# One core, two model blocks: another order of modulation, norms and first products, up to the attention heads

## The chip, the cores and the metric

The kernel runs as one program on one core of a Trainium2 chip. The metric is device time in microseconds, lower is better. Engines are named as in the profile: PE (TensorE, with PEld for its weight loads), ACT (ScalarE), DVE (VectorE), POOL (GpSimd), SP (SyncE, which issues all DMAs here).

## The reference, cut to what matters

The program runs two different blocks of a transformer on 256 tokens of width 1024, all in float32. Only the start of the first block is touched:

```python
sh1, sc1, g1, sh2, sc2, g2 = adaln(c, mod_w[0], mod_b[0])      # silu(c) @ mod_w + mod_b, 6 x 1024
csh1, csc1, *_ = adaln(c_ctx, mod_w[0], mod_b[0])
a  = rms_norm(x, g) * (1 + sc1) + sh1                          # 256 x 1024
ac = rms_norm(ctx, g) * (1 + csc1) + csh1                      # 256 x 1024
q, k, v, p = split(a @ w_in, [512, 640, 768])                  # 512, 128, 128, 512 wide
kc, vc = split(ac @ w_in[:, 512:768])                          # keys and values of the context
q = rope(rms_norm_per_head(q)); k = rope(rms_norm_per_head(k)); kc = rms_norm_per_head(kc)
y = concat(attend(q, [kc; k], [vc; v]), multiscale_pool(p)) @ w_out
x = x + g1 * y; x = x + g2 * hier_moe(modulate(x, sh2, sc2))
```

## The kernel before, in words

**Weights.** Every chunk of weights is 128 partitions x 2048 float32 (1 MiB; 0.5 MiB for a chunk of keys and values). SP walks the chunks in the order in which PE uses them and issues one DMA for each into a ring of seven slots (five during the heads); from the eighth chunk on each issue waits until PE has read the chunk that held the slot. Small inputs are issued at fixed places of that walk (`sync`, `c.n` is the number of the chunk).

**Exact products.** Apart from modulation, a product of a float32 activation with a float32 weight is done as three products of rounded parts (`mm3`): ACT writes the high part of the weights (`a_split`, tile `hi`), DVE or POOL subtracts it from the raw chunk to get the low part (`v_split`, `g_split`, tile `lo`), and the activation is split in the same way into `hTh` and `hTl` (for the context `yTh`, `yTl`). Chunks of `q` are subtracted on DVE, those of `kv` and `p` on POOL.

**Modulation.** A piece (layer, p) is 512 columns of `mod_w`: two chunks, 32 small products on PE into one bank (`t_mod`), a copy by ACT to `acc` (`a_mod`), a transposition back on PE (`t_mod_T`), and an addition of the bias on DVE (`v_mod`, for a gate `v_gate`). Pieces (0,0) to (0,3) are needed first; eleven others (`MODS0`) are computed between the products of the attention heads, step by step, in bank 3.

**A norm.** ACT squares and sums the rows (`a_stats`), DVE computes 1/rms by ten small steps on the tile `st` and puts it on a diagonal (`v_diag`), PE multiplies the input by that diagonal, which turns it too (`t_norm`), and DVE and ACT scale, shift and split the four result banks by turns (`v_norm`, `a_norm`; POOL takes one low part, `g_norm`).

**Order.** Every engine's program is written out by hand in `tensor`, `scalar`, `vector`, `gpsimd` (lines 3134 to 3312), and each engine executes strictly in order. Before, PE does modulation, the norm of x (`a0x`), the norm of the context (`a0c`), then the products kv, q, p, then turns queries and keys (`t_qk`) and enters the 16 heads (`t_heads0`). On DVE `v_keys0` (norm and rotation of the keys) stands ahead of `v_queries0`.

**Banks.** PSUM has eight banks. A product takes its banks by turns from a pool of banks (`POOLS`: A is 0 to 3, B is 4 to 7, S is 0 to 2). Its first product into a bank waits until the last reader of that bank has emptied it (`free`). All products of this stage came from pool B before: kv took banks 4 to 7, q banks 4 and 5, p banks 6 and 7.

Of the kernel before, what the change touches and what calls it, by code (L numbers as in the profile page):

```python
# [44 lines left out]
SMALL = ("sil", "cst", "col", "x", "cx", "row", "pos", "gb00", "gb01", "gb10", "gb11", "fg")  # L45
# [260 lines left out]
MODS0 = (0, 4), (0, 5), (0, 6), (0, 7), (0, 8), (0, 9), (1, 0), (1, 1), (1, 2), (0, 10), (0, 11)  # L306
EXTRA = {8: (1, 4), 10: (1, 5)}, {8: (1, 11)}
MODS = [(0, 0), (0, 1), (0, 2), (0, 3), *MODS0, (1, 3), *EXTRA[0].values(), (1, 6), (1, 7), (1, 8), (1, 9), (1, 10),
# [102 lines left out]
class Net(Tiles):  # L411
# [8 lines left out]
    def sync(self, s, book):  # L420
# [11 lines left out]
        for c in book.order:  # L432
            if c.n == 0:
                small("sil", self.sil[:, :], self.t_in["colp"][:, 160:176])
            elif c.n == 2:
                small("cst", self.cst[:, :], self.t_in["cst"])
            elif c.n == 4:
                small("col", self.col[:, :], self.t_in["colp"])
                small("x", self.x[:, :, :], self.t_in["x"])
                small("cx", self.cx, self.t_in["ctx"])  # L440
            elif c.n == 10:
                small("row", self.row[:, :], rows(0, RKEEP))
                small("pos", self.posi[:, :], self.t_in["pos"])
# [117 lines left out]
    def t_mod_T(self, t, l, p, pool="B"):  # L561
# [4 lines left out]
        t.wait_ge(*t.at("in", "cst"))  # L566
# [9 lines left out]
    def v_mod(self, v, l, p, cdst=None):  # L576
# [8 lines left out]
        v.wait_ge(*v.at("in", "col"))  # L585
# [65 lines left out]
    def v_diag(self, v, name, buf, c0):  # L651
        self.v_stats(v, name, c0)
        r = self.st[:, c0 + 4:c0 + 6]
        v.wait_ge(*v.at("in", "cst"))
# [259 lines left out]
    def a_queries0(self, a):  # L914

        for t in range(2):
            b = a.bank("q", t)
            a.wait_ge(*a.at("keys 0"))
# [37 lines left out]
    def a_qk(self, a):  # L956
        qT, kT = self.qk()
        a.wait_ge(*a.at("used", ("p", 1)))
# [172 lines left out]
    def t_mods0(self, t):  # L1131

        steps, late = None, []
        for n in range(self.STEPS0 + 6):
            for i in self.turn0(n):
# [4 lines left out]
                if i % 9 == 8:  # L1140
                    late.append((n + 2, piece))
# [12 lines left out]
    def v_mods0(self, v):  # L1154
        late = []
# [84 lines left out]
    def t_shift_of(self, t, l):  # L1240

        t.wait_ge(*t.at("scale", l, 1))
        b = t.take("B", "router shift", l)
# [20 lines left out]
    def t_route(self, t, l, src, beside):  # L1264
# [24 lines left out]
        gk = self.r3(64, 8)  # L1289
        t.wait_ge(*t.at("group marks", l))  # L1290
# [1843 lines left out]
    def tensor(self, t):  # L3134
# [37 lines left out]
    def scalar(self, a):  # L3172
        H, Y = self.H3, self.Y3
        self.a_silu(a)
        self.a_stats(a, "a0x", self.x, lambda h, t: a.at("in", "x"), self.s1, 0, ("sil",))
        self.a_stats(a, "a0c", self.cx, lambda h, t: a.at("in", "cx"), self.s2, 32)
        for p in range(4):
            self.a_mod(a, 0, p)
        self.a_split(a, "kv", 0, ahead=1)
        self.a_norm(a, "a0x", self.cadj[:, 3, :], self.mcol[:, 0:8], self.hT, H, [("scale", 0, 0)], [])  # L3180
        self.a_norm(a, "a0c", self.cadj[:, 2, :], self.cadj[:, 0, :], self.hTc(), Y, [("scale c",)], [])
        self.a_split(a, "kv", 1)
        self.a_split(a, "q", 1)
# [41 lines left out]
    def vector(self, v):  # L3225
        H, Y = self.H3, self.Y3
        self.v_silu(v)
        self.v_diag(v, "a0x", self.s1, 0)
        self.v_diag(v, "a0c", self.s2, 32)
        for p in range(4):  # L3230
            self.v_mod(v, 0, p, self.cadj[:, p // 2, 4 * (p % 2):4 * (p % 2) + 4])
        v.wait_ge(*v.last)
# [18 lines left out]
        self.v_queries0(v)  # L3251
# [3 lines left out]
        self.v_split(v, "eo", 0, 1, ahead=1)  # L3255
# [225 lines left out]
```

## Time and profile before

| | us |
|---|---|
| three runs | 1717.47, 1702.03, 1711.02 (median 1711.02) |
| profiled execution | 1706.65, of it span 1704.9 |
| first product of kv on PE | at 44.18 |
| turning of queries and keys on PE | at 79.06 |
| heads on PE | 81.38 to 172.13 |
| PE busy over the span | 93% |

Times inside the profiled execution are counted from the start of its span. The first block's attention ends at 172.13 us; the other 1530 us run code that the change doesn't touch. A row of the timeline gives the start, the time from the first start to the last end, the engine, the line, the tiles (out<-in), the number of instructions, and in brackets how long the engine had been idle before and what released it. Several rows of the same kind are merged.

### The profile page before, as it was taken

What the parts mean: (1) busy time and instruction counts of PE and PEld (TensorE: products, weight loads), DVE (VectorE), ACT (ScalarE), POOL (GpSimd) and SP (SyncE); (2) the same over time, 40 slices, a digit from 0 to 9 for tenths busy, and PEclk for the clock granted to TensorE, in tenths of its full rate; (3) what the DMA queues carried; (4) which work ended last, traced back from release to release, by engine and by line L of the source; (5) the groups of instructions that cost most, each with busy time, mean ns of one, the idle gap of its engine ahead of it and who ended that gap; (6) DMA issues with size and microseconds to landing.
All of it is one profiled execution on the core that took longest, in us unless ns stands there. A gap on an engine that the chain in (4) does not pass through costs nothing.

```text
span 1704.9 us, 23882 instructions
## 1 busy us (share of the span) xinstructions
PE 1588.9 (93%) x9950; PEld 1323.7 (78%) x9950; DVE 764.7 (45%) x1477; ACT 682.4 (40%) x1024; POOL 435.2 (26%) x163
## 2 busy tenths in 40 slices
PE   4999979999898899989999889999999998899997
PEld 4856867775797678668888668999888886789996
DVE  2722578422766774253352373522433522645222
ACT  3323367432435664233223344444432223354442
POOL 1200015330000343223100025655531000246543
PEclk7989889999998899999999999999999999999999
DMA  9578169769643696754433234555543332256550
GB/s 386 186 253 301 41 252 353 295 222 366 269 144 142 238 345 238 252 220 141 148 115 149 75 143 153 189 185 186 166 153 135 136 133 90 103 171 208 180 190 26
DMA packets 46620, 327.26 MB, mean 192 GB/s; under 512 B 5424, under 2 KB 5424, under 8 KB 8752
## 3 DMA queue, kind: packets, MB, share of 16 engines
q1 hardware_dynamic: 46512, 325.73, 53.0%
q8 instruction: 79, 1.29, 0.3%
q14 instruction: 29, 0.24, 0.0%
HBM read 324.66 MB, written 1.05 MB: 191 GB/s over the span
## 4 chain that ended last, share of the span: by engine, by line
PE 79%; DVE 13%; ACT 3%; DMA 2%; issue 1%; POOL 1%; DVEq 0%; SPq 0%; ACTq 0%
PE ps L201 28%; PE ps L204 16%; PE ps L206 16%; PE ps L205 16%; DVE lo L212 5%; DMA raw<-in_wmod 2%; ACT hi L209 1%; PE ps L2624 1%; DVE ar L212 1%; DVE big L220 1%; POOL lo L212 1%; DMA raw<-in_wo_v 1%; DVE gl L212 1%; DVE ar L2675 1%; DVE xn L212 0%
## 5 line engine op out<-in xcount | busy, mean ns | idle before, releaser
L212 POOL TENSOR_TENSOR lo<-raw,hi 128x2048 fp32r<-128x2048 f32 (+2 forms) x76 | 354.3, 4672 | 656.9 <-ACT hi L209 656.9
L209 ACT ACTIVATE hi<-raw 128x2048 fp32r<-128x2048 f32 (+2 forms) x192 | 350.8, 1858 | 47.5 <-PE ps L206 12.4
L212 DVE TENSOR_TENSOR lo<-raw,hi 128x2048 fp32r<-128x2048 f32 (+1 forms) x116 | 291.2, 2528 | 99.7 <-ACT hi L209 99.4
L201 PE MATMUL ps<-hT,raw 128*128 128x256 f32 x1024 | 231.4, 382 | 0.0
L201 PEld LDWEIGHTS ps<-hT,raw 128*128 128x128 f32 x1024 | 191.0, 190 | 29.6 <-issue 4.0
L204 PE MATMUL ps<-hTh,hi 128*128 128x256 f32 x640 | 183.1, 286 | 5.4 <-DVE hTl L212 2.9
L205 PE MATMUL ps<-hTl,hi 128*128 128x256 f32 x640 | 182.4, 285 | 0.0
L206 PE MATMUL ps<-hTh,lo 128*128 128x256 f32 x640 | 182.3, 285 | 0.0
L204 PEld LDWEIGHTS ps<-hTh,hi 128*128 128x128 f32 x640 | 124.1, 194 | 7.2 <-issue 3.5
L204 PE MATMUL ps<-hi,hTh 128*128 128x512 f32 (+3 forms) x320 | 119.5, 373 | 10.6 <-DVE hTl L212 5.2
L205 PEld LDWEIGHTS ps<-hTl,hi 128*128 128x128 f32 x640 | 124.1, 194 | 0.5
L206 PEld LDWEIGHTS ps<-hTh,lo 128*128 128x128 f32 x640 | 124.1, 194 | 0.0
L204 PE MATMUL ps<-hi,gh 128*128 128x512 f32 x256 | 106.5, 416 | 12.4 <-DVE lo L212 12.4
L206 PE MATMUL ps<-hi,hTl 128*128 128x512 f32 (+3 forms) x320 | 117.6, 367 | 0.0
L205 PE MATMUL ps<-lo,hTh 128*128 128x512 f32 (+3 forms) x320 | 117.4, 367 | 0.0
L212 POOL TENSOR_TENSOR big<-big 128x512 f32<-128x512 f32 x16 | 20.3, 1269 | 343.8 <-DVE big L220 343.8
L212 DVE TENSOR_TENSOR fTl<-s,fTh 128x512 fp32r<-128x512 f32 x32 | 22.1, 692 | 190.8 <-ACT fTh L209 190.8
L206 PE MATMUL ps<-hi,gl 128*128 128x512 f32 x256 | 103.6, 405 | 0.0
L205 PE MATMUL ps<-lo,gh 128*128 128x512 f32 x256 | 103.5, 404 | 0.0
L204 PE MATMUL ps<-hi,fTh 128*128 128x512 f32 x256 | 99.8, 390 | 0.0
L205 PE MATMUL ps<-lo,fTh 128*128 128x512 f32 x256 | 99.8, 390 | 0.0
L206 PE MATMUL ps<-hi,fTl 128*128 128x512 f32 x256 | 99.6, 389 | 0.0
(295 smaller groups left out, 2551.9 us busy)
## 6 DMA issues: line engine op xcount, KB each, us to landing
raw<-in_wgu SPq DMA_DIRECT2D x64, 1024.0 KB, 4.9
raw<-in_wmod SPq DMA_DIRECT2D x48, 1024.0 KB, 5.5
raw<-in_wdn SPq DMA_DIRECT2D x32, 1024.0 KB, 5.2
raw<-in_wgt SPq DMA_DIRECT2D x32, 1024.0 KB, 4.9
raw<-in_wup SPq DMA_DIRECT2D x32, 1024.0 KB, 4.7
raw<-in_wdown SPq DMA_DIRECT2D x32, 1024.0 KB, 5.1
raw<-in_wz SPq DMA_DIRECT2D x12, 1024.0 KB, 4.9
raw<-in_wbr SPq DMA_DIRECT2D x8, 1024.0 KB, 5.7
```

Source lines behind the costliest of these rows:

```text
L201: return self.e.matmul(o, l, r, start=first, stop=last)
L204: self.e.matmul(o, l[0], r[0], start=first, stop=False)
L205: self.e.matmul(o, l[0], r[1], start=False, stop=False)
L206: return self.e.matmul(o, l[1], r[0], start=False, stop=last)
L209: return self.e.activation(o, a, f, **kw)
L212: return self.e.tensor_tensor(o, a, b, op)
L220: return self.e.scalar_tensor_tensor(out=o, in0=a, scalar=s, in1=b, op0=op0, op1=op1)
L2624: m = t.e.transpose(ps[:, b, 128 * h:128 * h + 128], pb[:, n * h + 128 * kt:n * h + 128 * kt + 128], self.C("ident"))
L2675: o = v.e.tensor_tensor_reduce(pb[:, n * h:n * h + n], ps[:, b[h % 2], n * (h // 2):n * (h // 2) + n], mask(i, n), 1.0, -3e38, ALU.add, AL ...
```

## The change

Six things are moved, all in the first block:

1. Small inputs: only the identity (64 KB of `cst`) and the modulation's bias (80 KB of `col`) are loaded early, as `id` and `col0`; the rest of both is loaded after the chunks of kv, with the row constants and gates. The context (1 MiB, as x) is loaded at chunk 10.
2. ACT copies modulation pieces 0 and 1 before it squares x, and squares the context only after the second chunk of q is split; DVE's `v_diag` calls follow.
3. PE computes q directly after the norm of x, in banks 0 and 1 (pool A), then the norm of the context, then kv.
4. DVE does `v_queries0` before it copies the results of kv out of PSUM; `v_keys0` comes last. POOL splits the chunks of kv and p, DVE those of q.
5. Two gate pieces, (0,4) and (0,5), are computed by `t_mod` between p and `t_qk` (`AHEAD0`); `MODS0` keeps nine. Their transpositions stay in the heads.
6. After the heads DVE splits one chunk of the output weights before the last tail, not two, and the router's shift takes a bank of pool S.

```diff
-MODS0 = (0, 4), (0, 5), (0, 6), (0, 7), (0, 8), (0, 9), (1, 0), (1, 1), (1, 2), (0, 10), (0, 11)
+AHEAD0 = (0, 4), (0, 5)
+MODS0 = (0, 6), (0, 7), (0, 8), (0, 9), (1, 0), (1, 1), (1, 2), (0, 10), (0, 11)
...
             elif c.n == 2:
-                small("cst", self.cst[:, :], self.t_in["cst"])
+                small("id", self.cst[:, 0:128], self.t_in["cst"][:, 0:128])
+                small("col0", self.col[:, 0:160], self.t_in["colp"][:, 0:160])
             elif c.n == 4:
-                small("col", self.col[:, :], self.t_in["colp"])
                 small("x", self.x[:, :, :], self.t_in["x"])
+            elif c.n == 10:
                 small("cx", self.cx, self.t_in["ctx"])
-            elif c.n == 10:
+            elif c.n == 12:
+                small("cst", self.cst[:, 128:], self.t_in["cst"][:, 128:])
+                small("col", self.col[:, 160:], self.t_in["colp"][:, 160:])
                 small("row", self.row[:, :], rows(0, RKEEP))
...
     def tensor(self, t):
         self.t_norm(t, "a0x", self.x, self.s1)
+        both = [(H, ("hT", "a0x"), 0), (H, ("hT", "a0x"), 1)]
+        self.t_rows(t, ("q",), ("q",), 512, both, "A")
         self.t_norm(t, "a0c", self.cx, self.s2)
-        both = [(H, ("hT", "a0x"), 0), (H, ("hT", "a0x"), 1)]
         self.t_rows(t, ("kv",), ("kv",), 256, both + [(Y, ("hT", "a0c"), 0), (Y, ("hT", "a0c"), 1)])
-        self.t_rows(t, ("q",), ("q",), 512, both)
         self.t_rows(t, ("p",), ("p",), 512, both)
+        for piece in AHEAD0:
+            self.t_mod(t, *piece)
...
     def scalar(self, a):
         self.a_silu(a)
-        self.a_stats(a, "a0x", self.x, lambda h, t: a.at("in", "x"), self.s1, 0, ("sil",))
-        self.a_stats(a, "a0c", self.cx, lambda h, t: a.at("in", "cx"), self.s2, 32)
         for p in range(4):
             self.a_mod(a, 0, p)
+            if p == 1:
+                self.a_stats(a, "a0x", self.x, lambda h, t: a.at("in", "x"), self.s1, 0, ("sil",))
+        self.a_split(a, "q", 0, ahead=0)
+        self.a_norm(a, "a0x", self.cadj[:, 3, :], self.mcol[:, 0:8], self.hT, H, [("scale", 0, 0)], [])
+        self.a_split(a, "q", 1, ahead=0)
+        self.a_stats(a, "a0c", self.cx, lambda h, t: a.at("in", "cx"), self.s2, 32)
         self.a_split(a, "kv", 0, ahead=1)
-        self.a_norm(a, "a0x", self.cadj[:, 3, :], self.mcol[:, 0:8], self.hT, H, [("scale", 0, 0)], [])
         self.a_norm(a, "a0c", self.cadj[:, 2, :], self.cadj[:, 0, :], self.hTc(), Y, [("scale c",)], [])
-        self.a_split(a, "kv", 1)
-        self.a_split(a, "q", 1)
         self.a_queries0(a)
+        self.a_split(a, "p", 0, ahead=1)
...
     def vector(self, v):
+        self.v_split(v, "q", 0, ahead=0)
         self.v_norm(v, "a0x", self.cadj[:, 3, :], self.mcol[:, 0:8], self.hT, H, [("scale", 0, 0)], [])
+        self.v_split(v, "q", 1, ahead=0)
+        self.v_diag(v, "a0c", self.s2, 32)
         self.v_norm(v, "a0c", self.cadj[:, 2, :], self.cadj[:, 0, :], self.hTc(), Y, [("scale c",)], [])
         self.v_turns0(v)
-        self.v_split(v, "kv", 1)
         for k in range(4):
             v.wait_ge(*v.at("hT", "a0c", k))
+        self.v_queries0(v)
         for i in range(4):
             b = v.bank("kv", i)
...
         self.v_keys0(v)
-        self.v_queries0(v)
```

PE, the first product of each group with its waits, from the norm of the context to `t_qk`, before (`hi_83` and `hi_84` are kv's chunks, `hi_85` and `hi_86` q's, `hi_87` and the second `hi_83` p's; `free4` is bank 4):

```order
L204 MATMUL ps<-hi_83,hTh 128x256 [waits s_dve,s_free4,s_lo_pool]
...
L204 MATMUL ps<-hi_85,hTh 128x512 [waits s_free4,s_lo_dve]
...
L204 MATMUL ps<-hi_85,hTh 128x512 [waits s_free5]
...
L204 MATMUL ps<-hi_87,hTh 128x512 [waits s_free6,s_lo_pool]
...
L953 MATMUL ps<-cst,z 128x128 [waits s_dve,s_free4]
```

The same engine and place now (`hi_83` and `hi_84` are q's chunks, `hi_85` and `hi_86` kv's, `hi_87` p's first):

```order
L204 MATMUL ps<-hi_83,hTh 128x512 [waits s_dve,s_lo_dve]
...
L201 MATMUL ps<-s_65,z 128x128 [waits s_free4,s_dve]
...
L204 MATMUL ps<-hi_85,hTh 128x256 [waits s_free4,s_lo_pool]
...
L204 MATMUL ps<-hi_87,hTh 128x512 [waits s_free4,s_lo_pool]
...
L204 MATMUL ps<-hi_87,hTh 128x512 [waits s_free5]
...
L201 MATMUL ps<-raw_69,sil 32x128 [waits s_raw0,s_free6]
...
L957 MATMUL ps<-cst,z 128x128 [waits s_dve,s_free4]
```

q waits for no bank any more, and p, which follows kv directly, now waits for banks 4 and 5, the two that kv has just filled.

DVE, from the rotation tables to the last keys or queries, before:

```order
L212 TENSOR_TENSOR rt<-cst,row 128x4x16 x2
L212 TENSOR_TENSOR lo_79<-raw_72,hi_85 128x2048
L212 TENSOR_TENSOR lo_80<-raw_73,hi_86 128x2048
L223 COPY z<-ps 128x256 x4
L212 TENSOR_TENSOR s_62<-z 128x256 x2
L226 TENSOR_REDUCE st<-s_62 128x4 x2
...
L212 TENSOR_TENSOR s_65<-ps,rt 128x512
L212 TENSOR_TENSOR s_65<-ps,rt 128x8x16 x4
L212 TENSOR_TENSOR z<-s_65 128x512
```

And now:

```order
L212 TENSOR_TENSOR rt<-cst,row 128x4x16 x2
L212 TENSOR_TENSOR s_65<-ps,rt 128x512
L212 TENSOR_TENSOR s_65<-ps,rt 128x8x16 x4
L212 TENSOR_TENSOR z<-s_65 128x512
...
L226 TENSOR_REDUCE st<-s_62 128x8 x2
...
L216 TENSOR_SCALAR st<-st 128x16 x2
L223 COPY z<-ps 128x256 x4
L212 TENSOR_TENSOR s_62<-z 128x256 x2
```

The four copies `z<-ps` empty the banks of kv. They stood directly behind the split of q's chunks; now all of `v_queries0` stands ahead of them.

## Rows read from the trace of the kernel before

**Rows 1.** Stages by windows: PE, PEld, DVE, ACT, POOL busy, PE clock, DMA share, GB/s.

```profile
0.00:44.18 44.18, 21.07 (x325) 17.51 (x325) 12.57 (x49) 14.46 (x33) 7.02 (x7) 0.81 0.96 387
44.18:79.06 34.88, 34.88 (x193) 31.07 (x194) 29.19 (x67) 13.17 (x15) 11.36 (x3) 0.95 0.57 208
81.38:172.13 90.75, 85.46 (x996) 55.48 (x996) 21.89 (x54) 28.59 (x66) 0.00 (x0) 0.92 0.79 267
```

**Rows 2.** The chain that ended last, start and duration, up to the first kv product.

```profile
1.20 5.48 DMA raw<-in_wmod
...
8.79 24.52 DMA raw<-in_wmod
...
42.41 1.76 issue
```

**Rows 3.** DMA issues of the first 150 us: size, median time to landing.

```profile
col<-in_colp SPq DMA_DIRECT2D x1, 803.0 KB, 13.5
cst<-in_cst SPq DMA_DIRECT2D x1, 568.0 KB, 8.5
```

**Rows 4.** ACT by timeline: squares of x, modulation copies, high parts.

```profile
20.92 0.63 ACT L209 ACTIVATE s<-x 128x512 f32<-128x512 f32 x1 [18.12 <-DMA x<-in_x]
...
26.68 0.42 ACT L209 ACTIVATE acc<-ps 128x128 f32<-128x128 f32 x2
...
48.51 7.31 ACT L209 ACTIVATE hi<-raw 128x2048 fp32r<-128x2048 f32 x4
```

**Rows 5.** DVE by timeline: the norm of x, q's low parts.

```profile
36.17 1.00 DVE L217 TENSOR_SCALAR hT<-ps,cadj,mcol 128x256 f32<-128x256 f32 x2 [0.46 <-PE ps L201]
37.93 0.79 DVE L212 TENSOR_TENSOR hTl<-hT,hTh 128x512 fp32r<-128x512 f32 x1 [0.76 <-ACT hTh L209]
...
50.45 4.50 DVE L212 TENSOR_TENSOR lo<-raw,hi 128x2048 fp32r<-128x2048 f32 x2 [0.64 <-ACT hi L209]
```

**Rows 6.** PE by timeline: the context's norm, two products of p.

```profile
38.58 3.83 PE L201 MATMUL ps<-s,z 128*128 128x128 f32 x32
...
72.02 0.39 PE L206 MATMUL ps<-hi,hTl 128*128 128x512 f32 x1
...
78.82 0.39 PE L206 MATMUL ps<-hi,hTl 128*128 128x512 f32 x1
```

**Rows 7.** DVE and POOL by timeline, where both work at once.

```profile
54.10 10.08 POOL L212 TENSOR_TENSOR lo<-raw,hi 128x2048 fp32r<-128x2048 f32 x2 [6.42 <-ACT hi L209]
...
57.46 0.42 DVE L223 COPY z<-ps 128x256 f32<-128x256 f32 x1 [1.02 <-PE ps L206]
58.02 6.44 DVE L212 TENSOR_TENSOR s<-z 128x256 f32<-128x256 f32 x2
...
1076.40 9.50 POOL L212 TENSOR_TENSOR lo<-raw,hi 128x2048 fp32r<-128x2048 f32 x2 [4.36 <-ACT hi L209]
...
1076.76 4.58 DVE L212 TENSOR_TENSOR st<-st 128x2 f32<-128x2 f32 x1
1081.38 4.55 DVE L217 TENSOR_SCALAR st<-st 128x2 f32<-128x2 f32 x1
```

**Rows 8.** DVE by timeline: second query tile, reductions, last factors.

```profile
73.92 1.48 DVE L212 TENSOR_TENSOR s<-ps,rt 128x512 f32<-128x512 f32 x5
...
76.04 1.27 DVE L226 TENSOR_REDUCE st<-s 128x8 f32<-128x512 f32 x2
...
79.44 0.25 DVE L216 TENSOR_SCALAR st<-st 128x16 f32<-128x16 f32 x2
```

**Rows 9.** Windows with PE at half its clock.

```profile
44.00:48.00 4.00, 3.82 (x19) 3.85 (x20) 2.61 (x5) 3.74 (x8) 1.28 (x1) 0.57 1.01 426
...
109.00:123.00 14.00, 14.00 (x114) 8.10 (x106) 2.02 (x6) 3.21 (x7) 0.00 (x0) 0.51 0.49 163
```

**Rows 10.** PE in the heads, by form and by timeline: modulation's products.

```profile
L201 PE MATMUL ps<-raw,sil 128*32 128x128 f32 x704 | 30.5, 295 | 5.3 <-ACT acc L209 5.3
...
86.05 1.52 PE L201 MATMUL ps<-raw,sil 128*32 128x128 f32 x48
```

More of the change, by code:

```diff
@@ L44 @@
 SEMS.update({f"raw{r}": f"a chunk of weights landed in slot {r}" for r in range(NR)})
-SMALL = ("sil", "cst", "col", "x", "cx", "row", "pos", "gb00", "gb01", "gb10", "gb11", "fg")
+SMALL = ("sil", "id", "cst", "col0", "col", "x", "cx", "row", "pos", "gb00", "gb01", "gb10", "gb11", "fg")
 SEMS.update({f"in_{k}": f"{k} landed" for k in SMALL})
@@ L301, in source @@
     return part(t_in["wdown"][at[0], at[1]], at[2]), "pool"
-MODS0 = (0, 4), (0, 5), (0, 6), (0, 7), (0, 8), (0, 9), (1, 0), (1, 1), (1, 2), (0, 10), (0, 11)
+AHEAD0 = (0, 4), (0, 5)
+MODS0 = (0, 6), (0, 7), (0, 8), (0, 9), (1, 0), (1, 1), (1, 2), (0, 10), (0, 11)
 EXTRA = {8: (1, 4), 10: (1, 5)}, {8: (1, 11)}
-MODS = [(0, 0), (0, 1), (0, 2), (0, 3), *MODS0, (1, 3), *EXTRA[0].values(), (1, 6), (1, 7), (1, 8), (1, 9), (1, 10),
+MODS = [(0, 0), (0, 1), (0, 2), (0, 3), *AHEAD0, *MODS0, (1, 3), *EXTRA[0].values(), (1, 6), (1, 7), (1, 8), (1, 9), (1, 10),
         *EXTRA[1].values()]
@@ L565, in t_mod_T @@
         t.wait_ge(*t.empty("mod", l, p))
-        t.wait_ge(*t.at("in", "cst"))
+        t.wait_ge(*t.at("in", "id"))
         t.wait_ge(*t.free(b))
@@ L584, in v_mod @@
         pv = self.ps[:, b, 0:128].rearrange("p (q w) -> p q w", q=4)
-        v.wait_ge(*v.at("in", "col"))
+        v.wait_ge(*v.at("in", "col0"))
         v.wait_ge(*v.full("mod T", l, p))
@@ L653, in v_diag @@
         r = self.st[:, c0 + 4:c0 + 6]
-        v.wait_ge(*v.at("in", "cst"))
+        v.wait_ge(*v.at("in", "id"))
         v.wait_ge(*v.last)
@@ L917, in a_queries0 @@
             b = a.bank("q", t)
-            a.wait_ge(*a.at("keys 0"))
+            a.wait_ge(*a.at("diag used", "a0x"))
             a.wait_ge(*a.full("q", t))
@@ L957, in a_qk @@
         qT, kT = self.qk()
-        a.wait_ge(*a.at("used", ("p", 1)))
+        a.wait_ge(*a.at("used", ("mod", *AHEAD0[-1], 1)))
         for i in (5, 4, 0, 1, 2, 3):
@@ L1075, in t_pool0 @@
         t.wait_ge(*t.at("landed", c.key))
+        t.wait_ge(*t.at("in", "col"))
         for g in range(0, 4, 2):
@@ L1131, in t_mods0 @@
     def t_mods0(self, t):
-        steps, late = None, []
+        steps, late = None, [(2 + i, piece) for i, piece in enumerate(AHEAD0)]
         for n in range(self.STEPS0 + 6):
@@ L1140, in t_mods0 @@
                 if i % 9 == 8:
-                    late.append((n + 2, piece))
+                    late.append((n + 3, piece))
             for at, piece in late:
@@ L1154, in v_mods0 @@
     def v_mods0(self, v):
-        late = []
+        late = [(2 + i, piece) for i, piece in enumerate(AHEAD0)]
         for n in range(self.STEPS0 + 6):
@@ L1242, in t_shift_of @@
         t.wait_ge(*t.at("scale", l, 1))
-        b = t.take("B", "router shift", l)
+        b = t.take("B" if l else "S", "router shift", l)
         rw = self.K("rw", 160 * l, 160).rearrange("p (k n) -> p k n", k=8)
@@ L1289, in t_route @@
         gk = self.r3(64, 8)
+        t.wait_ge(*t.at("in", "cst"))
         t.wait_ge(*t.at("group marks", l))
@@ L3188, in scalar @@
             a.ac(self.z[:, t, 768:1280], self.ps[:, b, :]).then_inc(*a.up(f"free{b}"))
+        for piece in AHEAD0:
+            self.a_mod(a, *piece)
         self.a_qk(a)
@@ L3227, in vector @@
         self.v_silu(v)
-        self.v_diag(v, "a0x", self.s1, 0)
-        self.v_diag(v, "a0c", self.s2, 32)
         for p in range(4):
             self.v_mod(v, 0, p, self.cadj[:, p // 2, 4 * (p % 2):4 * (p % 2) + 4])
+            if p == 1:
+                self.v_diag(v, "a0x", self.s1, 0)
         v.wait_ge(*v.last)
@@ L3254, in vector @@
         self.v_shares0(v, 1)
-        self.v_split(v, "eo", 0, 1, ahead=1)
+        self.v_split(v, "eo", 0, 1, ahead=0)
         self.v_tail0(v, 1)
@@ L3285, in gpsimd @@
         H, Y = self.H3, self.Y3
+        self.g_norm(g, "a0x", self.hT, H)
         self.g_split(g, "kv", 0, ahead=1)
-        self.g_norm(g, "a0x", self.hT, H)
         self.g_norm(g, "a0c", self.hTc(), Y)
-        self.g_split(g, "kv", 1)
-        self.g_split(g, "q", 1)
+        self.g_split(g, "p", 0, ahead=1)
         self.g_moe(g, 0, "a1")
```

## The prediction

> **What bounds the kernel now.** I read the windows first, cut at the places where PE's work changes kind, then the chain of waits from the start, then the timelines of ACT, DVE, POOL and PE. The change touches only the time up to 172.13 us. Three stages lie in it [rows 1]. Up to 44.18 us PE is busy for 21 of 44 us and the DMA engines for 0.96: this stage waits for weights. From 44.18 to 79.06 us (kv, q, p) PE is busy without a gap. In the heads, 90.75 us, PE is busy for 85.5. So the first stage can be shortened by loading less, the second only by removing work or by starting it earlier, the third by removing PE's work. After 172.13 us nothing is moved but one split on DVE and one bank, and I expect no difference there.
>
> The chain says what starts the second stage: the last modulation chunk lands at 8.79 + 24.52 = 33.3 us, PE works on it and on two norms, and then stands for 1.76 us [rows 2]. That stand is the wait for bank 4, which DVE empties late.
>
> **Part 1, loads.** The first chunk landed at 6.7 us, the eighth at 33.3 [rows 2], and with four small inputs (x and the context among them, 1 MiB each) 10.3 MiB lay between them: 2.57 us per MiB. Ahead of the eighth chunk the change removes 504 KB of constants and 723 KB of columns [rows 3] and 1024 KB of context, 2.2 MiB: it should land at 27.7 us, 5.6 us earlier, and q's first chunk, now next in line, at 30.2. ACT no longer holds the modulation copies behind eight squares (20.92 to 26.68 us [rows 4]); that alone is worth nothing, as the copies still wait for the last chunk. The constants that come late (keys' and queries' tables) follow kv's chunks: 4.1 + 2.57 for each of the 15.2 MiB up to the row constants is 43 us, and they are first used near 61. No cost; if that cover went, DVE's `v_turns0` would stand.
>
> **Part 2, the start of q.** High part of q's first chunk 1.83 us (a quarter of 7.31 [rows 4]), low part 2.25 (half of 4.50), DVE's scaling and split of the first bank 2.55 (36.17 to 38.72 [rows 5]): 30.2 + 6.6 = **36.8 us**, against 44.18 for kv before. Gain so far 7.4 us.
>
> **Part 3, q.** From 72.02 to 78.82 us PE started 30 products [rows 6]: 0.227 us each, 48 are 10.9 us. The stand before it will cost clock: before, PE stood 1.76 us and then showed a granted clock of 0.57 from 44 to 48 us [rows 2, 9], half speed (1.2 instead of 2.4 GHz) for about 3.4 us, so 1.7 us lost. I take the same here: q ends at 36.8 + 12.6 = 49.4.
>
> **Part 4, the context's norm, which now stands between q and kv.** ACT ends x's norm about 5.6 us after DVE began it (39.9), splits q's second chunk (1.83) and squares the context (eight squares took 5.76 us [rows 4], four 2.9): 44.7 us. DVE then needs ten small steps and two diagonals, 2.7 us, so 47.4, ahead of the end of q. But ACT's next work is the high parts of kv, and POOL starts to subtract about 1.1 us later, at 45.8, twice 2.5 us. Here rows 7 decide. At 58.02 us two DVE operations that read two SBUF tiles took 6.44 us, where their kind needs 0.3 each; POOL's two subtractions ended at 64.18. At 1076.76 us a step on two columns took 4.58 us and the next one 4.55, one for each of POOL's two subtractions, while the copy out of PSUM at 57.46 took 0.42 under the same load. So each POOL subtraction lets one DVE step through and holds the next to its end. Ten small steps against two subtractions: the diagonal comes at 45.8 + 5.1 + 1.2 = 52.1 us, and PE stands **2.7 us**. Then the norm, 3.83 us [rows 6] and 1.7 for the clock after the stand: 57.6. Then kv, 96 products of half the columns, 11.5 us: 69.1. The bounds of the stand are 0 (DVE done before POOL begins) and 5.1 (both subtractions in full).
>
> The Trainium skill (SBUF — State Buffer, "SBUF: two separate sides") states the same as an exclusive lock between VectorE and GpSimd, held for a whole instruction, for VectorE operations with two SBUF inputs or in a 2-port mode. By it a reduction of one tile in float32 would pass under POOL. No row shows one under load; I let it pass, and otherwise 1.3 us [rows 8] would have to be added below.
>
> **Part 5, the wait of p for its banks.** This is the largest term. PE's rows show that p now takes banks 4 and 5, just filled by kv, and DVE's rows that the copies which empty them stand behind `v_queries0`. DVE ends the context's low parts at 60.7 us and the tables at 61.3. Queries: tile 0 2.2 us (63.5), products of tile 1 1.5 us (65.0) [rows 8]. ACT has meanwhile squared q and written p's high part (61.1 + 1.8), and POOL's two subtractions of p, 4.5 us each when alone (9.50 for two [rows 7]), run from 63.5 to about 68.0 and, after DVE has slipped in once (0.7), to 73.1. DVE: the addition of tile 1 waits to 68.0, ends 68.7; reductions 1.3, 70.0; the first step on `st` waits to 73.1; the rest 2.4 us (77.31 to 79.69 before), 75.5; the first copy 0.4: **75.9 us**. PE finished kv at 69.1, so it stands 6.8 us. Bounds: without the lock DVE is there at 69.8 (0.7 us of standing); with the reductions held too, 8.1. I take the middle, as rows 7 show the same operations on the same POOL chunks. p: 10.9 + 1.7 for the clock, 88.5. p's low parts (73.1) are there in time.
>
> **Part 6, the two pieces.** 48 products of modulation took 1.52 us [rows 10], or 64 for a piece 2.0 us: 4.0 us more ahead of `t_qk`, **92.5** against 79.06, +13.4. Keys (7 us of DVE from 77) are done by 85. In the heads the same 4.0 us go, and of four stands behind ACT's copy of bank 3, 5.3 us [rows 10], which hit the pieces whose last step falls into the first third of a round, three are left: -1.3. Half-speed stretches there (109 to 123 us [rows 9]) I leave as they are. The first chunk for the heads is requested when (0,4) has been used, about 10 us before it is needed, and lands in some 5.5. DVE's split of the second output chunk moves behind the tail and is needed 5 us later than it is ready: nothing.
>
> **Sum.** From q's start to `t_qk`: q 12.6, stand 2.7, norm 5.5, kv 11.5, stand 6.8, p 12.6, pieces 4.0, together 55.7 us, against 34.9 before: +20.8. Less 7.4 for the earlier start: +13.4. Less 5.3 in the heads: **+8.1 us**. Against the profiled execution, 1706.65, that is 1714.8. The median of the three runs lies 4.4 above it, the mean of all four times 2.7 above; I say **1716**.
>
> **The rivals.** (B) DVE is through in time: POOL's subtractions of p come late or let DVE through, and p starts with 0.7 us of standing. Less 6.1 and 1.7 of clock: +0.3, about 1707 to 1711. For it: a shift of 2 us in ACT's order is enough to separate the two engines. Against: both start from the same event, the end of the context's norm. (C) Faster: neither stand occurs (-2.7 and -1.7 more, so -4), and the stretch of 14 us at half clock in the heads, which began soon after a stand of 1.6 us, doesn't come, as fewer stands are left: -7. Together -11, 1696 to 1700. It decides if no PE stand over 1.1 us is left in the heads: the ones of that length did not bring the clock down. (D) Slower: the stand of p lasts 8.1 us and the half clock after it 14 us, as in the heads [rows 9], not 3.4: 1.3 and 5.3 more, +14.7, 1721 to 1726. It decides if p's products are still at half speed when the pieces begin. (E) The heads don't shorten, because each round is bound by the chain score, maximum, exponential and not by PE: +4 on the forecast, 1720. Against it: in rows 1 PE idles only 5.3 of 90.75 us, all named.
>
> **How the numbers follow.** Forecast 0.50, B 0.24, C 0.10, D 0.09, E 0.07. One per cent is 17 us, about what a measurement tells from no change; all cases but the ends of C and D lie within it: faster 0.03, same 0.91, slower 0.06. The runs of before spread over 15 us, and the range takes in B, E and most of D: 1703 to 1725.
>
> **What would show it.** Right: q's first product near 37 us; a DVE step on `st` of over 2 us near 46 to 51; PE idle 5 to 8 us ahead of p's first product, ended by a DVE copy `z<-ps`; `t_qk` near 92; heads about 5 us shorter. Wrong: q later than 40 (loads not bound by bytes), no gap ahead of p (B), a heads stage as long as before (E).

## The result, and the profile after

The changed kernel takes **1715.11 us** (median of 19 runs, 1704.7 to 1741.23); the kernel before, run beside it, 1705.32 (19 runs, 1695.37 to 1717.47). The ratio is 1.0053 (95%: 1.0034 to 1.0073): half a per cent slower, inside the one per cent called no change, at the place forecast (1716). Every ratio here and in the table below leaves out runs more than 1.5% above the fastest of their kernel (three of the changed kernel's 19, up to six of twelve below); medians, ranges and means have all runs. The profiled execution took 1709.32 us, of it span 1707.5, against 1706.65 and 1704.9.

The first rows are those of the start: DMA and ACT in the chain of waits, and PE's timeline (start, duration, what, and in brackets the idle time before and its releaser).

```profile
1.67 7.55 DMA raw<-in_wmod
...
11.25 19.07 DMA raw<-in_we_q
30.35 1.92 ACT hi L209
```

```profile
27.88 1.08 PE L201 MATMUL ps<-raw,rt 128*32 128x128 f32 x32 [1.02 <-DMA raw<-in_wmod]
...
37.08 0.77 PE L204 MATMUL ps<-hi,hTh 128*128 128x512 f32 x1 [3.82 <-DVE hTl L212]
...
44.27 0.50 PE L204 MATMUL ps<-hi,hTh 128*128 128x512 f32 x1 [0.15 <-DVE lo L212]
...
51.91 3.84 PE L201 MATMUL ps<-s,z 128*128 128x128 f32 x32 [1.87 <-DVE s L216]
...
75.64 0.77 PE L204 MATMUL ps<-hi,hTh 128*128 128x512 f32 x1 [8.38 <-DVE z L223]
...
89.15 3.70 PE L201 MATMUL ps<-raw,sil 128*32 128x128 f32 x128
92.78 1.62 PE L957 MATMUL ps<-cst,z 128*128 128x128 f32 x12
94.89 3.69 PE L201 MATMUL ps<-raw,z 128*128 128x256 f32 x16 [0.48 <-ACT big L209]
...
178.34 1.91 PE L201 MATMUL ps<-col,mcol 128*128 128x20 f32 x16
```

The eighth chunk is used at 27.88 (33.3 before, [rows 2]), q's first chunk lands at 30.3, q starts at 37.08. Then come two stands (stretches in which PE waits): 1.87 us ahead of the context's norm, ended by the diagonal (`s`), and 8.38 us ahead of p, ended by a copy `z<-ps`. `t_qk` is at 92.78, the heads end at 178.34; before, 79.06 and 172.13.

DVE under those two stands, and POOL beside it (same columns):

```profile
45.80 2.41 DVE L212 TENSOR_TENSOR st<-st 128x2 f32<-128x2 f32 x1
48.24 2.31 DVE L220 SCALAR_TENSOR_TENSOR st<-st 128x2 f32<-128x2 f32 x1
50.59 0.16 DVE L212 TENSOR_TENSOR st<-st 128x2 f32<-128x2 f32 x1
...
61.68 4.99 DVE L212 TENSOR_TENSOR z<-s 128x512 f32<-128x512 f32 x1
66.80 1.48 DVE L212 TENSOR_TENSOR s<-ps,rt 128x512 f32<-128x512 f32 x5
68.32 3.28 DVE L212 TENSOR_TENSOR z<-s 128x512 f32<-128x512 f32 x1
71.52 1.27 DVE L226 TENSOR_REDUCE st<-s 128x8 f32<-128x512 f32 x2
...
75.08 1.41 DVE L223 COPY z<-ps 128x256 f32<-128x256 f32 x4
```

```profile
45.79 4.75 POOL L212 TENSOR_TENSOR lo<-raw,hi 128x1024 fp32r<-128x1024 f32 x2 [6.65 <-ACT hi L209]
...
61.49 9.55 POOL L212 TENSOR_TENSOR lo<-raw,hi 128x2048 fp32r<-128x2048 f32 x2 [3.77 <-ACT hi L209]
```

This is the pattern of [rows 7] again. One step on two columns normally takes 0.16 us (the row at 50.59); while POOL's two small subtractions ran, two such steps took 2.41 and 2.31. Ahead of p two additions, one for each of POOL's large subtractions, took 4.99 and 3.28.

By windows (PE, PEld, DVE, ACT, POOL busy, then PE clock, DMA share, GB/s):

```profile
0.00:44.00 44.00, 25.71 (x316) 19.95 (x316) 12.97 (x36) 15.60 (x30) 1.48 (x5) 0.88 0.96 388
...
66.00:76.00 10.00, 1.62 (x12) 1.44 (x11) 9.45 (x24) 0.00 (x0) 5.05 (x2) 0.73 0.31 106
75.00:79.00 4.00, 3.36 (x8) 2.71 (x9) 3.68 (x14) 0.00 (x0) 0.00 (x0) 0.50 0.01 4
...
178.00:1707.50 1529.50, 1441.38 (x8432) 1215.02 (x8431) 703.28 (x1304) 623.83 (x906) 414.74 (x153) 0.97 0.51 182
```

In the first 44 us PE now does 25.7 us of work instead of 21.1 [rows 1]. In ten microseconds around the second stand it does 1.6, and the granted clock after it is 0.50 (1.2 GHz). The span moved less than the heads' end (2.6 against 6.2 us): the stage behind the heads, in which only one split and one bank were moved, took 1529.2 us instead of 1532.8. Windows at the same place behind the heads say why, first before, then after:

```profile
174.00:181.00 7.00, 6.39 (x18) 4.77 (x17) 6.96 (x7) 4.92 (x4) 0.00 (x0) 0.51 0.31 126
```

```profile
180.00:187.00 7.00, 6.25 (x31) 5.06 (x31) 6.97 (x7) 4.71 (x4) 0.00 (x0) 1.00 0.36 136
```

Seven microseconds at the same place, before at half clock, now at full clock (18 products against 31): about 3.5 us. I don't count them for the change: in the fourteen profiled executions of the table below the stage behind the heads took 1528.5 to 1538.1 us, and in the eight that have the changed code there 1528.5 to 1535.7. With one execution of each this is likely, not shown.

Every run also has a mean granted clock for its whole span. A straight line through the 19 runs of the changed kernel falls by 14.6 us for each 0.01 of clock and explains 97% of the variance (46 to 73% in the three groups of the kernel before). Read at one clock, 0.965, the changed kernel is at **1716.0** and the kernel before, from the 99 executions that ran beside the experiments (lines with 9 to 11 us for 0.01), at 1705.9, 1706.7 and 1707.7. That is the column "at 0.965" below; it is a reading aid worked out from the runs, good to about a microsecond or two. Where a kernel itself brings more half clock, the column takes that away as well: it tells what an order of work costs, not what a run takes.

### The profile page after: what moved, and what is told of

Read it like the earlier page. It is cut to its first block, busy times and chain, and to the rows that moved or that the text cites. A ratio compares the mean times of both kernels' runs of the same rounds, so it can differ in the third digit from the quotient of the medians.

```text
span 1707.5 us, 23884 instructions
## 1 busy us (share of the span) xinstructions
PE 1585.6 (93%) x9950; PEld 1319.6 (77%) x9950; DVE 772.5 (45%) x1477; ACT 683.0 (40%) x1024; POOL 431.8 (25%) x163
## 4 chain that ended last, share of the span: by engine, by line
PE 77%; DVE 15%; ACT 4%; DMA 2%; issue 1%; POOL 1%; DVEq 0%; SPq 0%; ACTq 0%
PE ps L201 27%; PE ps L204 16%; PE ps L206 15%; PE ps L205 15%; DVE lo L212 5%; ACT hi L209 1%; DMA raw<-in_we_q 1%; PE ps L2630 1%; DVE ar L212 1%; DVE big L220 1%; DVE z L212 1%; POOL lo L212 1%; DMA raw<-in_wo_v 1%; ACT hTh L209 1%; DVE s L212 1%
## 5 line engine op out<-in xcount | busy, mean ns | idle before, releaser
L209 ACT ACTIVATE hi<-raw 128x2048 fp32r<-128x2048 f32 (+1 forms) x192 | 351.0, 1858 | 48.2 <-PE ps L201 12.6
```

The source lines that it names most:

```text
L209: return self.e.activation(o, a, f, **kw)
```

## The experiments

My theory: two locks of DVE behind POOL make two stands; p's stand is made by a bank that `v_queries0` holds; at the heads two pieces less save what they cost ahead. The rival readings: the order of DVE's work alone, without POOL, costs the time; the stands are hidden anyway; or it is the pieces. The kernels ran in three groups; the kernel before had medians of 1703.96, 1706.39 and 1707.58 us beside them. Nothing is left out of the computation in any of them.

| kernel | median, us | ratio to before (95%) | span | end of heads | at 0.965 | clock up to 0.955 |
|---|---|---|---|---|---|---|
| before | | 1 | 1704.9 | 172.13 | 1706 to 1708 | 1 of 99 |
| after | 1715.11 | 1.0053 (1.0034-1.0073) | 1707.5 | 178.34 | 1716.0 | 3 of 19 |
| e1 | 1706.29 | 1.0004 (0.9971-1.0037) | 1698.9 | 166.55 | 1710.1 | 1 of 12 |
| e2 | 1717.25 | 1.0077 (1.0046-1.0108) | 1705.0 | 171.95 | 1714.4 | 2 of 12 |
| e3 | 1717.01 | 1.0102 (1.0046-1.0158) | 1715.5 | 179.94 | 1717.0 | 1 of 6 |
| e4 | 1709.97 | 1.0033 (1.0007-1.0059) | 1703.9 | 171.57 | 1707.8 | 0 of 12 |
| e5 | 1701.39 | 0.9995 (0.9960-1.0031) | 1695.7 | 167.19 | 1706.2 | 3 of 12 |
| e6 | 1701.95 | 0.9970 (0.9940-1.0001) | 1697.4 | 160.97 | 1703.9 | 4 of 12 |
| e7 | 1712.47 | 1.0046 (1.0018-1.0074) | 1729.7 | 195.26 | 1710.6 | 4 of 12 |
| e8 | 1712.11 | 1.0045 (1.0015-1.0075) | 1709.4 | 173.74 | 1714.2 | 0 of 12 |
| e9 | 1708.37 | 1.0019 (0.9994-1.0045) | 1705.1 | 172.29 | 1705.8 | 0 of 12 |
| e10 | 1707.44 | 1.0013 (0.9990-1.0035) | 1707.1 | 172.56 | 1708.8 | 0 of 12 |
| e11 | 1715.24 | 0.9988 (0.9949-1.0027) | 1701.2 | 163.11 | 1701.9 | 6 of 12 |
| e12 | 1704.50 | 0.9967 (0.9932-1.0003) | 1696.6 | 162.49 | 1703.4 | 4 of 12 |

**e1: p in other banks.** The wait for banks 4 and 5 is taken away, DVE and POOL are left as they are.

```diff
-        self.t_rows(t, ("p",), ("p",), 512, both)
+        self.t_rows(t, ("p",), ("p",), 512, both, "A")
         for piece in AHEAD0:
-            self.t_mod(t, *piece)
+            self.t_mod(t, *piece, "A")
```

> The changed kernel with one edit: p's products take banks 2 and 3, and the two pieces behind them banks 0 and 1, so that PE waits for no copy of kv's banks. Theory (the wait of p for its banks costs 8.4 us, 67.3 to 75.6, and 1.7 us of clock): p starts within 1 us of the end of kv, near 67.5; p and the pieces end near 82, where t_qk now waits for the keys, which DVE ends at 83.8 as in the changed kernel; heads on PE start near 86 instead of 94.9. So 8 to 9 us faster than the changed kernel, level with the kernel before or up to 3 us better (ratio 0.998 to 1.000). Rival (the stand is the low part of p on POOL, or queries that PE would wait for anyway): p still starts after 71, and the gain is under 4 us. Rival (half clock in the heads is what costs): t_qk moves, the end doesn't.

PE and DVE by timeline:

```profile
51.95 3.84 PE L201 MATMUL ps<-s,z 128*128 128x128 f32 x32 [1.66 <-DVE s L216]
...
78.14 3.70 PE L201 MATMUL ps<-raw,sil 128*32 128x128 f32 x128
...
84.06 1.60 PE L957 MATMUL ps<-cst,z 128*128 128x128 f32 x12 [2.22 <-DVE z L212]
```

```profile
61.72 4.98 DVE L212 TENSOR_TENSOR z<-s 128x512 f32<-128x512 f32 x1
...
68.36 3.37 DVE L212 TENSOR_TENSOR z<-s 128x512 f32<-128x512 f32 x1
...
75.21 1.41 DVE L223 COPY z<-ps 128x256 f32<-128x256 f32 x4
```

DVE is as late as before (copies at 75.21), but p no longer waits: the pieces start at 78.14, 11.0 us earlier, which is the stand of 8.4 us and the 2.6 us that half clock took behind it. What is late next is DVE's keys: `t_qk` waits 2.22 us. The bank, not p's data, made the stand. At equal clock this is 6 us of the 9.

**e2: p's low parts on DVE.** POOL is idle while DVE does the queries.

```diff
-        return part(...), "dve" if name == "q" else "pool"
+        return part(...), "pool" if name == "kv" else "dve"
...
             v.wait_ge(*v.empty("kv", i))
+        self.v_split(v, "p", 0, ahead=1)
         self.v_keys0(v)
```

(and POOL's `g_split` of p goes)

> The changed kernel with the low parts of p subtracted on DVE behind the copies of kv's banks, and not on POOL. It tests the lock by itself: POOL is idle while DVE rotates the queries. Theory (DVE operations on two SBUF tiles wait for POOL's subtraction): the two additions z<-s take 0.7 us each instead of 4.99 and 3.28, v_queries0 takes 8.2 us instead of 14.9, kv's copies stand at 67.5 to 69.5 instead of 75.1, and p starts near 72, when its first low part is written: 3 to 4 us faster than the changed kernel, still 2 to 6 us slower than before. Rival (the additions are slow for another reason, such as ACT writing the same banks): they stay at 3 to 5 us, p starts later than 76 and the kernel is slower than the changed one.

```profile
62.82 0.69 DVE L212 TENSOR_TENSOR z<-s 128x512 f32<-128x512 f32 x1
65.16 0.69 DVE L212 TENSOR_TENSOR z<-s 128x512 f32<-128x512 f32 x1
...
69.33 1.41 DVE L223 COPY z<-ps 128x256 f32<-128x256 f32 x4
70.98 4.49 DVE L212 TENSOR_TENSOR lo<-raw,hi 128x2048 fp32r<-128x2048 f32 x2 [0.23 <-DVE z L223]
```

Both additions fall to 0.69 us: POOL's subtractions were what held them. The copies come 5.75 us earlier, p starts at 73.32, now waiting for its low part, and `t_qk` comes at 89.43, 3.4 us earlier. The gain shows in the trace and at equal clock (-1.6), not in the median (1717.25): the runs spread from 1704 to 1740. Expected were 2 to 6 us above before; the medians say 13, equal clock 8.5.

**e3: the pieces back in the heads**, all else as changed.

```diff
-AHEAD0 = (0, 4), (0, 5)
-MODS0 = (0, 6), (0, 7), (0, 8), ...
+AHEAD0 = ()
+MODS0 = (0, 4), (0, 5), (0, 6), (0, 7), (0, 8), ...
```

(with it, ACT's copies behind `t_qk` wait for p's last product and not for the pieces', and PE passes over two banks behind the heads, so that the banks there stay as changed)

> The changed kernel with the two modulation pieces (0,4) and (0,5) back in the heads (eleven pieces there, none ahead), all else as changed. Theory (the pieces' 3.6 us move from the heads to the stretch ahead of them, and lighter rounds lose one stand): t_qk 3.6 us earlier, near 89.1, heads 83.5 plus 4 to 7 us; in all 0 to 3.5 us slower than the changed kernel. Rival (filler was free in the heads and costs 3.6 us ahead of them): 3.6 us faster than the changed kernel, heads still 83 to 85 us.

`t_qk` comes 3.8 us earlier (88.94) and the heads last 89.2 us, 5.8 longer: the end of the heads is 1.6 us later than with the change. But PE was at half clock for 10.2 us of these heads against 6.8 in the changed kernel's, which is 1.7 us: without it both traces end at the same place, and moving the pieces gained nothing in them (the rows had given -1.3). Six runs don't fix it in the medians.

**e4: the early loads alone**, in the kernel before, with its order kv, q, p.

```diff
         for p in range(4):
             self.v_mod(v, 0, p, ...)
+            if p == 1:
+                self.v_diag(v, "a0x", self.s1, 0)
+                self.v_diag(v, "a0c", self.s2, 32)
```

(beside it the loads `id` and `col0` as in the change, the rest of `cst` and `col` at chunk 10 ahead of the row constants, and ACT's copies of pieces 0 and 1 ahead of the squares)

> The kernel before with the first part of the change alone: identity and modulation bias loaded early, the rest of both constants with the row constants, ACT's modulation copies 0 and 1 ahead of the squares; the context stays where it was, and so do all products. Theory (the first stage is bound by the bytes ahead of the eighth chunk): 1227 KB less ahead of it at 2.57 us per MiB, it lands at 30.2 instead of 33.3, kv starts near 41.1 instead of 44.18, and all behind it moves by 3.1 us: ratio to before 0.998, 1702.2 against 1705.3. Rival (what bounds kv is DVE and POOL on the norms): kv starts at 43 or later, no difference.

The eighth chunk is used at 30.30, about 3 us earlier than before, but kv starts at 44.88 (44.18 before): nothing of it arrives. DVE and POOL show why:

```profile
32.62 2.58 DVE L216 TENSOR_SCALAR s<-cst,st 128x128 f32<-128x128 f32 x2
...
35.51 1.94 DVE L220 SCALAR_TENSOR_TENSOR cadj<-cadj,col 128x8 f32<-128x8 f32 x1
```

```profile
32.75 4.67 POOL L212 TENSOR_TENSOR lo<-raw,hi 128x1024 fp32r<-128x1024 f32 x2 [32.30 <-ACT hi L209]
```

My own edit put the second diagonal (0.48 us alone) under POOL's subtractions. The context's scale, 0.17 us alone, took 1.94 behind it. So the 3.1 us by which the data came earlier were lost to 2.1 + 1.8 us of lock, and the rival reading put on record (kv is bound by DVE and POOL, whatever the loads do) held for this kernel. **e9** moves the two `v_diag` calls one place up (`p == 0`):

```diff
-            if p == 1:
+            if p == 0:
                 self.v_diag(v, "a0x", self.s1, 0)
```

> e6_loads_pieces without its two pieces ahead: the kernel before with the loads moved, ACT's first copies ahead of the squares and DVE's two diagonals behind modulation piece 0; eleven pieces in the heads. What is open: the kernels with nine pieces in the heads have runs far above their median (e6_loads_pieces: eight of 12 between 1696 and 1707 us, four between 1726 and 1731; in the trace of e7_copies_first PE stood at half clock from 112.8 to 170.8 us of the heads), the kernel before none in 83. Theory (the lighter rounds let PE fall to half clock for long): here kv starts near 41.3, heads end 3 us earlier than before (169), all runs lie within 12 us of the median, median 1701 to 1703, 0.997 to 0.999 of before. Rival (the far runs come from the loads or by chance): runs above 1722 here as well.

kv then starts at 41.17, 3.0 us ahead of before. At equal clock it takes 1705.8, 0 to 2 less than before; the ratio is 1.0019 with 1 inside the interval, and the median, 1708.37, missed the 1701 to 1703 expected. So the gain shows in the trace (`t_qk` at 74.66 against 79.06) and in no time of a run. In this profiled execution the end of the heads was not earlier (172.29) because 24 us in them were at half clock, against 13.7 before.

**e8: POOL waits for the diagonal.**

```diff
         self.g_norm(g, "a0x", self.hT, H)
+        g.wait_ge(*g.at("diag", "a0c"))
         self.g_split(g, "kv", 0, ahead=1)
```

> The changed kernel with one wait more on POOL: its two subtractions of kv stand behind the context's diagonal. Theory (the stand of 1.9 us ahead of the context's norm is POOL holding two of DVE's ten small steps, 2.41 and 2.31 us): the ten steps take 0.16 to 0.17 us each, the diagonal comes at 47.5, the norm starts within 0.3 us of the end of q. POOL ends kv's second low part near 52.5, before it is needed. The stand of p for its banks moves 1.9 us forward and stays 8 us: 2 us faster than the changed kernel. Rival (the steps are slow for another reason): the norm still starts near 51.9.

The first stand is gone: PE goes from q into the norm at 49.96 (51.91), p starts at 73.58 after the same 8.38 us of standing. Of the 1.95 us 1.6 are carried through to `t_qk` (91.21 against 92.78).

**e7: the copies ahead of the queries on DVE.**

```diff
-        self.v_queries0(v)
         for i in range(4):
...
             v.cp(self.z[:, i % 2, c0:c0 + 256], self.ps[:, b, 0:256]).then_inc(*v.up(f"free{b}"))
+        self.v_queries0(v)
```

> The changed kernel with DVE's four copies of kv's banks ahead of v_queries0 again, all else as changed. Theory (p waits for nothing but those copies): the copies come at 67.5 to 69, p starts near 67.9 instead of 75.6, but the queries' chain starts only at 69, behind it 8 us, of which POOL's second subtraction holds up to 2.5, then the keys, 7 us: DVE ends near 86 to 87, where t_qk waits, against 92.8 in the changed kernel. So heads start 6 us earlier than in the changed kernel, 2 to 3 later than in e1_p_bank; level with before within 3 us. Rival (p's start is bound by POOL's low parts): p starts after 70.

```profile
63.16 0.43 DVE L223 COPY z<-ps 128x256 f32<-128x256 f32 x1 [3.24 <-PE ps L206]
...
67.38 0.42 DVE L223 COPY z<-ps 128x256 f32<-128x256 f32 x1 [1.01 <-PE ps L206]
69.46 1.88 DVE L212 TENSOR_TENSOR z<-s 128x512 f32<-128x512 f32 x1
...
72.99 0.69 DVE L212 TENSOR_TENSOR z<-s 128x512 f32<-128x512 f32 x1
```

Copies out of PSUM pass under POOL (0.42 and 0.43 us, POOL busy from 61.58 to 70.79), p has its banks at once, and the pieces start at 78.18, as in e1. DVE is the later of the two at `t_qk`, which waits 2.81 us (84.69). This profiled execution has a long half-clock stretch in the heads (below); only its positions ahead of the heads are compared.

**e5: all stands mended**: e1's banks, e8's wait, and p's low parts on DVE between the rotation of the queries and their factors.

```diff
             v.mark("queries 0", t)
+        self.v_split(v, "p", 0, ahead=1)
         st = self.st
```

> The changed kernel with all its stands taken away: p in banks 2 and 3 and the pieces in 0 and 1 (as in e1_p_bank), p's low parts on DVE between the rotation of the queries and their factors, and POOL's subtractions of kv behind the context's diagonal. Theory (both stands of PE are the shared access of DVE and POOL, the second through the banks): the context's norm starts within 0.3 us of the end of q (near 50), kv ends near 65.5, p starts at once, t_qk near 80 (DVE ends the keys near 79.5), heads on PE start near 82: 4 us earlier than in e1_p_bank (86.1), 13 earlier than in the changed kernel. In all 10 to 13 us faster than the changed kernel, 0.998 to 0.995 of before. Rival (once the stands are gone, the timed runs lose the gain to half clock in the heads, as e1_p_bank, whose heads ended 5.6 us earlier than before in its trace and whose median was 2 us above): heads end 8 us earlier in the trace, the median within 3 us of before.

```profile
46.08 0.16 DVE L212 TENSOR_TENSOR st<-st 128x2 f32<-128x2 f32 x1
...
59.97 0.69 DVE L212 TENSOR_TENSOR z<-s 128x512 f32<-128x512 f32 x1
```

PE now works from q to the heads with no stand but the usual 0.48 us ahead of the heads; the pieces start at 76.39, `t_qk` at 80.02, 12.8 us earlier than in the change and 1.0 later than before, with two pieces more done. At equal clock 1706.2: 10 us less than the change, and back at the time of before (mean of all runs 1705.7, before 1706.0). The 0.998 to 0.995 of before that was expected is not reached.

**e10: e5 with the pieces back in the heads** (edit as in e3).

> e5_all_mended with the two pieces back in the heads: q first, both stands taken away, no work moved ahead. Theory: p ends near 76.4, t_qk waits for the keys on DVE until 79.6, so nothing is gained over e5_all_mended ahead of the heads, and the heads are 3.5 to 4 us longer: heads end near 169 to 171 with the same clock, median 1701 to 1705, but no run above 1722. Rival (the far runs belong to q's order): runs above 1722 here as well.

Without the pieces `t_qk` comes at 79.69, after a wait of 3.27 us for DVE's keys, hardly earlier than in e5 (80.02): there the two pieces fill a wait and cost 0.3 us. The heads end at 172.56, later than e5's by 5.4 us, of which 1.7 is half clock in the heads (13.6 us long against 10.2), and at equal clock it takes 1708.8, 2.6 more than e5. Both the end of the heads and the median (1707.44) lie above what was expected.

**e6, e12: the good halves on the old order** (kv, q, p as before; loads; `v_diag` as in e9; two pieces ahead in banks 0 and 1). e12 is the same kernel, run again in another group.

```diff
         self.t_rows(t, ("p",), ("p",), 512, both)
+        for piece in AHEAD0:
+            self.t_mod(t, *piece, "A")
```

> The kernel before with the loads of e4_loads_only, DVE's two diagonals directly behind modulation piece 0 (in e4_loads_only they stood behind piece 1 and ran into POOL's subtractions of kv: 2.58 us for two diagonals, 1.94 for the scale), and the two pieces (0,4), (0,5) ahead of t_qk, in banks 0 and 1. q, kv and p stay in their order of before. Theory: scale ready near 32.3, kv starts near 41 instead of 44.2 (e4: 44.9), t_qk near 79.6, heads 3 to 7 us shorter: heads end near 166, 0.996 to 0.998 of before. Rival (kv's start is bound by bank 4 and DVE whatever the loads do): kv starts after 43, all in all level with before.

> e6_loads_pieces once more, unchanged, beside e9_loads_diag and e11_dense_filler on one chip. Theory: again most runs between 1696 and 1707 us and one to five of 12 above 1722; median 1698 to 1704. Rival (chance): none above 1722.

In e6 kv starts at 41.25, the pieces at 74.82, `t_qk` at 78.45, and in e6 and e12 the heads end at 160.97 and 162.49, 10 to 11 us earlier than before. Both medians are below the one of before beside them and both intervals just reach 1: 0.9970 (0.9940 to 1.0001) and 0.9967 (0.9932 to 1.0003). The trace of e6 gains 7.5 us of span, the medians 3 to 4. The rest is in the runs: eight of these 24 lie at 1720 us or above, with a clock of 0.952 or less, and only one of the 99 of before has a clock as low as 0.955. Over all runs, these eight with them, the means are 1709.5 and 1708.4, against 1706.0 and 1706.4 beside them: on average the early loads and the pieces gain nothing.

**e11: the remaining pieces packed into fewer steps.** One reading of those long runs: with nine pieces over 48 steps the heads are too thin for the clock.

```diff
-        return range(n * m // self.STEPS0, (n + 1) * m // self.STEPS0) if n < self.STEPS0 else ()
+        return range(n * m // 40, (n + 1) * m // 40) if n < 40 else ()
```

> e6_loads_pieces with the nine pieces spread over the first 40 of the heads' 48 steps and not over all 48, so that a round holds as much modulation as in the kernel before (2.03 steps against 2.06) until round 13; the last rounds have none. Theory (PE falls to half clock for long where the rounds are light): fewer far runs than in e12_loads_pieces_again, if they come, from the last rounds alone, so at most 6 us above the rest; median within 2 us of it. Rival (density has nothing to do with it): as many runs above 1722 as there.

Six of twelve runs at a clock of 0.953 or less, against eight of 24: denser filling didn't help, and this reading fell (the median of all twelve, 1715.24, is 7.7 above before).

## Why the prediction was right

**Loads.** Forecast: eighth chunk at 27.7, q's at 30.2, q's first product at 36.8. Measured 27.9, 30.3, 37.08. The rate of 2.57 us per MiB held.

**q and the first stand.** The lock with two steps held was as forecast, 4.7 us for both. The diagonal came at 51.85 (said 52.1). The stand was 1.87 instead of 2.7, since q took 13.0 us (said 12.6) and ended at 50.05 and not 49.4; half clock took 1.4 of it, near the 1.7 counted. The half clock counted after this stand didn't come: the norm took 3.84, not 5.5. kv ended at 67.3, not 69.1. e8 shows that this stand is the lock's.

**The wait of p.** The mechanism of the largest term came as described: DVE held by POOL, then reductions, factors, copies, and the bank. What was held did not. The forecast let the first addition pass and had POOL, from 63.5 to 73.1, hold the second one and a step on `st`; POOL began at 61.49 and held both additions (4.99, 3.28), and no step on `st`. It was through 2.1 us earlier than said, but the reductions (1.3 us), which were to pass under it, came behind. That the end of the stand was right to 0.3 us (75.64, said 75.9) is therefore in part luck. Its length was undersized, 8.4 instead of 6.8, since kv ended 1.8 us earlier while DVE's chain, which sets the end, did not. e2 and e5 show the lock, e1 and e7 the bank. One assumption stays open: that a reduction would pass under POOL. They began at 71.52, when POOL had ended (71.04), so none shows one under load, nor does any other reduction in this trace or in that of before. Of the Trainium skill's rule (SBUF — State Buffer, "SBUF: two separate sides"), that VectorE with two SBUF inputs is locked out while GpSimd works, the rows agree (0.69 against 4.99); the copy out of PSUM passed (0.42).

**Pieces and `t_qk`.** Pieces 3.7 (said 4.0), `t_qk` 92.78 (said 92.5).

**Heads.** The forecast was -5.3, measured -7.3 (83.45 against 90.75). This is not a better effect of the pieces: half-clock stretches in the heads were 6.8 us long (about 124.9 to 131.8, see the window), not 13.7, which is 3.4 us. The rest, 3.9, is the mechanism, so this term was too large by 1.4. The window, and PE's waits in the heads (total us, times, longest):

```profile
125.00:132.00 7.00, 7.00 (x55) 3.83 (x54) 1.01 (x3) 1.47 (x3) 0.00 (x0) 0.52 0.49 165
```

```profile
PE ps L201 <- ACT acc L209: 3.7, 5, 1.1
PE ps L201 <- ACT big L209: 1.4, 2, 0.9
```

Together 5.1, against 5.3 before [rows 10]: the stand that should go was replaced by shorter ones, so only the two pieces' own work counts. At full clock all through, e6 shows what heads with nine pieces take (windows):

```profile
80.56:160.97 80.41, 75.83 (x867) 48.55 (x868) 22.05 (x54) 28.90 (x64) 0.00 (x0) 1.00 0.81 286
```

**Sum.** From q's start to `t_qk` 55.7 us were said and 55.7 measured, with misses that cancel: the norm 1.9 and the first stand 0.8 shorter, the stand of p 1.6 and p itself 0.9 longer, the rest smaller. +8.1 was said. The end of the heads moved by 6.2 in the profiled executions, and by 9.6 with the heads' half clock taken as equal (3.4 added). At equal clock the runs give +8 to +10. The medians differ by 9.8 and the means by 13.0, in part by lower clocks in the changed kernel's runs (mean 0.963 against 0.966). The 1716 itself is in part luck: it puts the kernel before at 1707.9, 2.6 above its median of 19 runs, and the difference 1.7 below the measured one.

**The rivals.** B (p starts with hardly a stand) is what e1, e7 and e5 make by hand; it did not occur by itself, as POOL began both times within the same 0.2 us as DVE's step. C fell with the stands. Its sign in the heads was no guide either: no wait there was longer than 1.1 us, and half clock came all the same, 1 us behind one of 1.10. D fell: p's products were at half clock from 75.6 to 80.9 (2.6 us lost, where 1.7 was counted and D has 7) and at full clock long before the pieces began. E fell, the heads did shorten.

## What to carry to other kernels

An order that brings an engine's input 7 us earlier can lose 17 us behind it (55.7 us instead of 34.9 up to `t_qk`, of which 3.7 are the pieces): follow the first wait of each group that is moved, including the bank it takes and the work that stands ahead of that bank's last reader. Where DVE and POOL both work on SBUF, place DVE's small steps before POOL's long subtractions begin, or give POOL a wait for them (e8: one line, 1.6 us at `t_qk`). And compare profiled executions at the same clock before calling a few microseconds a gain, since here each 0.01 of mean clock is some 7 to 16 us (the lines through the runs of each kernel).

## What the runs showed of the hardware that was not expected

**The clock in the heads.** Moving two pieces ahead takes about 4 us of PE's work out of the heads, but such kernels more often have a run at a clock of 0.955 or less (a bound that I set after seeing the runs): 27 of 115 runs in the nine rows of the table with nine pieces in the heads, 2 of 141 in the five with eleven, or 1 of 42 without the kernel before. Three pairs differ in this alone. e6 and e12 together have 8 of 24 against e9's 0 of 12, e5 has 3 of 12 against e10's 0 of 12 (suggestive only), but the changed kernel has 3 of 19 against e3's 1 of 6, which shows nothing. So that the pieces are the cause is likely, not shown. One profiled execution, e7's, caught one:

```profile
112.00:119.00 7.00, 5.90 (x66) 3.17 (x65) 0.85 (x2) 2.12 (x7) 0.00 (x0) 0.92 0.85 290
...
119.00:176.00 57.00, 57.00 (x391) 32.52 (x390) 8.96 (x23) 13.18 (x29) 0.00 (x0) 0.50 0.47 152
```

From about 118 to 176 us (e9's expectation has it at 112.8 to 170.8, which is too early) PE is busy without any gap, and at 1.2 GHz. That costs 29 us, so one stretch like this explains a run 25 to 30 us above the others. A few microseconds before it PE had stood once for 1.10 us; e6, with no such stretch, has stands of the same length. What sets it off stays open: filling as thin as e6's, which e11 undid, is not it, and e3, with eleven pieces, had one such run of six. That the far runs of the other kernels have the same cause in the same place is likely from their clock, but was seen in this one trace only.

**Stands and clock.** 1.76 us of standing before kv was followed by half clock in the kernel before [rows 2, 9], 1.87 us ahead of the norm in the changed one was not, and in e2, 1.90 us was: the norm took 5.47 us there.

```profile
51.92 5.47 PE L201 MATMUL ps<-s,z 128*128 128x128 f32 x32 [1.90 <-DVE s L216]
```

A stand alone doesn't decide it. The forecast counted 1.7 us for each of three stands, 5.1 in all; the changed kernel's trace gives 1.4, 0 and 2.6, 4.0 in all.
